# A two-block transformer kernel: the second key unit's copy-out moved ahead, eight vector products regrouped between VectorE and GpSimd, GpSimd's products cut into 512-column pieces

## The reference

```python
mod_lat = jnp.split(jax.nn.silu(c) @ w_ada[l] + b_ada[l], 6, axis=-1)
mod_ctx = jnp.split(jax.nn.silu(c_ctx)[None, :] @ w_ada[l] + b_ada[l], 6, axis=-1)
pl = project(modulate(rmsnorm(x, g_mix[l]), sh1, sc1), w_in[l], w_dec_up[l], b_dec[l])
pc = project(modulate(rmsnorm(ctx, g_mix[l]), sh1c, sc1c), w_in[l], w_dec_up[l], b_dec[l])
o_c, s_cf, s_cb = gla_bidir(pc[0], pc[1], pc[2], pc[4], pc[5], zeros_state, zeros_state)
o_l, _, _ = gla_bidir(pl[0], pl[1], pl[2], pl[4], pl[5], s_cf, s_cb)
mix_l = merge_branches(o_l, pl[3], pl[6], ...)
x = x + gt1[:, None, :] * mix_l
x = x + gt2[:, None, :] * swiglu(modulate(rmsnorm(x, g_ffn[l]), sh2, sc2), ...)
```

## Time and profile before

| | us |
|---|---|
| median of 3 runs | 1207.5 (1204.62 to 1208.31) |
| profiled execution, its own time | 1210.52 |
| span of the profiled execution | 1208.5 |
| TensorE matmul busy | 1135.7 (94%) |
| VectorE busy | 861.6 (71%) |
| ScalarE busy | 569.5 (47%) |
| GpSimd busy | 325.1 (27%) |

### The profile page before, as it was taken

One profiled execution on the slowest core, in us unless ns is written; L12 is line 12 of the kernel. 1 busy time (PEld: TensorE's weight loads), 2 busy tenths in 40 slices (PEclk: granted clock), 3 DMA queues, 4 the chain that ended last, 5 costly groups with the idle time before them and its releaser, 6 DMA issues.

```text
span 1208.5 us, 19055 instructions
## 1 busy us (share of the span) xinstructions
PE 1135.7 (94%) x7764; PEld 1027.4 (85%) x7764; DVE 861.6 (71%) x944; ACT 569.5 (47%) x729; POOL 325.1 (27%) x226
## 2 busy tenths in 40 slices
PE   2968999999999999999989999999999989999996
PEld 2968988999998988888878888889998989888885
DVE  1579474488678678787778887788666687755676
ACT  3464434443442464444455444446655635544452
POOL 4077563165756100000020000011257663000000
PEclk8988989999999899999989999999999999999999
DMA  9932645466785658777737777756954565656670
GB/s 288 295 129 90 194 131 164 121 216 213 235 284 170 227 171 277 243 249 247 281 132 266 253 248 249 263 165 197 296 178 148 187 206 174 209 180 203 212 258 35
DMA packets 192547, 250.28 MB, mean 207 GB/s; under 512 B 4859, under 2 KB 171966, under 8 KB 192350
## 3 DMA queue, kind: packets, MB, share of 16 engines
q1 hardware_dynamic: 183838, 216.92, 55.3%
q0 software_dynamic: 8640, 32.38, 7.9%
HBM read 248.23 MB, written 1.05 MB: 206 GB/s over the span
## 4 chain that ended last, share of the span: by engine, by line
PE 75%; DVE 14%; ACT 4%; issue 4%; SPq 2%; DMA 1%; POOL 0%; POOLq 0%; DVEq 0%; ACTq 0%
PE twin L1286 73%; DVE arena L1892 5%; DVE wlo L1892 4%; ACT arena L864 2%; DVE arena L1900 2%; ACT whi L864 1%; DVE X L1892 1%; DMA arena<-in_w_ada 1%; PE twin L1347 1%; DVE arena L2175 1%; SPq L512 1%; PE twin L1612 0%; DVE X L1900 0%; SPq L562 0%; DVE arena L1896 0%
## 5 line engine op out<-in xcount | busy, mean ns | idle before, releaser
L1286 PE MATMUL twin<-A_both,whi 128*128 128x256 f32 (+1 forms) x2208 | 580.1, 340 | 1.5 <-DVE arena L1892 1.1
L1892 DVE TENSOR_TENSOR wlo<-raw,whi 128x2048 fp32r<-128x2048 f32 x169 | 420.2, 2487 | 144.5 <-ACT whi L864 144.3
L1286 PE MATMUL twin<-A_both,wlo 128*128 128x256 f32 x1632 | 437.0, 281 | 0.0
L864 ACT ACTIVATE whi<-raw 128x2048 fp32r<-128x2048 f32 x169 | 323.2, 1912 | 209.2 <-PE twin L1286 209.2
L1286 PEld LDWEIGHTS twin<-A_both,whi 128*128 128x128 f32 x2208 | 371.3, 190 | 44.7 <-issue 6.9
L1286 PEld LDWEIGHTS twin<-A_both,wlo 128*128 128x128 f32 x1632 | 309.9, 190 | 11.4 <-DVE A_both L1892 0.6
L1286 PE MATMUL twin<-whi,A_both 128*128 128x256 f32 x640 | 124.5, 296 | 27.5 <-ACT arena L864 15.2
L864 ACT ACTIVATE arena<-arena 128x512 f32<-128x512 f32 (+7 forms) x132 | 70.1, 558 | 167.9 <-DVE arena L1892 132.9
L864 ACT ACTIVATE arena<-twin 128x512 f32<-128x512 f32 (+5 forms) x167 | 88.4, 555 | 116.6 <-PE twin L1286 85.7
L779 POOL TENSOR_TENSOR ada_raw<-ada_raw,arena 128x2048 f32<-128x2048 f32 x24 | 98.1, 4089 | 136.7 <-DMA ada_raw<-in_w_ada 136.7
L1286 PEld LDWEIGHTS twin<-whi,A_both 128*128 128x128 f32 x640 | 105.4, 202 | 29.7 <-issue 16.2
(11 more groups left out here) (134 smaller groups left out, 1213.6 us busy)
## 6 DMA issues: line engine op xcount, KB each, us to landing
raw<-in_w_in SPq DMA_DIRECT2D x48, 1024.0 KB, 5.7
raw<-in_ffn_w_in SPq DMA_DIRECT2D x44, 1024.0 KB, 5.1
ada_raw<-in_w_ada POOLq DMA_DIRECT2D x28, 1024.0 KB, 6.2
ada_raw<-in_w_ada SPq DMA_DIRECT2D x24, 1024.0 KB, 5.4
raw<-in_w_ffn_in SPq DMA_DIRECT2D x22, 1024.0 KB, 5.1
raw<-in_ffn_w_out SPq DMA_DIRECT2D x22, 1024.0 KB, 4.9
raw<-in_w_ffn_out SPq DMA_DIRECT2D x11, 1024.0 KB, 5.1
arena<-in_w_ada SPq DMA_DIRECT2D x8, 1024.0 KB, 11.6
```

The costliest lines, as they stand in the source:

```text
L864: return nc.scalar.activation(o, i, f, **kw)
L1286: return nc.tensor.matmul(o, l, r, start=start, stop=stop, **kw)
L1892: return nc.vector.tensor_tensor(o, x, y, op)
```

## The change

Five edits, all in block one.

1. ScalarE copies out unit 2 (`evac1(U_K + 1)`) in round 2, between `decays(1)` and `log_decays(2)`, no longer in round 3.
2. Pieces 0 and 1 of the modulation products go to VectorE (`ADA_DVE`), in its rounds 4 and 5.
3. GpSimd still loads piece 0 at the same place, then loads piece 1 when VectorE is through with piece 0, piece 2 when it is through with piece 1, and only then computes, pieces 2 to 7.
4. On GpSimd the product of a block-one piece is 4 instructions of 512 columns, and the first sum 2 of 512.
5. VectorE does `decayed_queries` behind the second `gla_step` of rounds 8 and 9, so behind `add_state`.

```diff
--- before.py
+++ after.py
@@ -120,7 +120,7 @@
 
 ADA_FFN = [n for n in range(len(ADA)) if NADA1 <= n < ADA_P2 or n >= ADA_LAST]
 ADA_MIX = [n for n in range(len(ADA)) if n not in ADA_FFN]
-ADA_DVE = [n for n in range(len(ADA)) if n in ADA_FFN or ADA_P2 <= n < ADA_P2 + 4]
+ADA_DVE = [n for n in range(len(ADA)) if n < 2 or n in ADA_FFN or ADA_P2 <= n < ADA_P2 + 4]
 ADA_POOL = [n for n in range(len(ADA)) if n not in ADA_DVE]
 
 LAST_STEPS = (0, NF - 4, NF - 3, NF - 2)
@@ -776,8 +776,16 @@
                 dst = acc[:, UC * ada_pos(n):UC * ada_pos(n) + UC]
                 pool.wait_ge(*ada_landing(n))
                 v = ada_raw
-                link(nc.gpsimd.tensor_tensor(v[:], v[:], c3[:, :, s:s + 1].to_broadcast([P, KD, UC]), ALU.mult))
-                link(nc.gpsimd.tensor_tensor(v[:, 0:4, :], v[:, 0:4, :], v[:, 4:8, :], ALU.add))
+                step = 2 if n < NADA1 else 8
+                for k in range(0, KD, step):
+                    ins = nc.gpsimd.tensor_tensor(v[:, k:k + step, :], v[:, k:k + step, :],
+                                                  c3[:, k:k + step, s:s + 1].to_broadcast([P, step, UC]), ALU.mult)
+                link(ins)
+                step = min(step, 4)
+                for k in range(0, 4, step):
+                    ins = nc.gpsimd.tensor_tensor(v[:, k:k + step, :], v[:, k:k + step, :], v[:, k + 4:k + 4 + step, :],
+                                                  ALU.add)
+                link(ins)
                 link(nc.gpsimd.tensor_tensor(v[:, 0:2, :], v[:, 0:2, :], v[:, 2:4, :], ALU.add))
                 nc.gpsimd.tensor_tensor(dst, v[:, 0, :], v[:, 1, :], ALU.add).then_inc(ada_sum, 1)
 
@@ -814,10 +822,11 @@
             norm(0)
             norm(1)
             load_ada(0)
-            pool.wait_ge(hlo_done, 16)
-            for n in range(8):
+            load_ada(1)
+            for n in range(2, 8):
+                load_ada(n)
                 adapt(n)
-                load_ada(n + 1)
+            load_ada(8)
             for t in range(TT):
                 pool.wait_ge(osq_done, t + 1)
                 root(orstd[:, 4 * t:4 * t + 4], oss[:, 4 * t:4 * t + 4], HV).then_inc(orstd_done, 1)
@@ -1049,6 +1058,7 @@
                 if u == U_K + 1:
                     decays(0)
                     decays(1)
+                    evac1(U_K + 1)
                     log_decays(2)
                     soft_part(2)
                 if u == U_V:
@@ -1247,8 +1257,9 @@
             split(2)
 
             for u in range(N1):
+                if u and u != U_K + 2:
+                    evac1(u - 1)
                 if u:
-                    evac1(u - 1)
                     split(u + 2)
                 gla_front(u)
                 gla_step(2 * (u - 1 - U_Q) + 1)
@@ -2228,8 +2239,6 @@
                 if u == U_V:
                     for g in range(4):
                         decayed_keys(g)
-                if u in (U_Q + 1, U_Q + 2):
-                    decayed_queries(u - U_Q - 1)
 
             def gla_step(slot):
 
@@ -2517,6 +2526,11 @@
                     split(u + 2)
                 gla_front(u)
                 gla_step(2 * (u - U_Q))
+                if u in (U_Q + 1, U_Q + 2):
+                    decayed_queries(u - U_Q - 1)
+                if u in (U_V + 1, U_V + 2):
+                    n = u - U_V - 1
+                    adapt(n, 0, acc[:, UC * ada_pos(n):UC * ada_pos(n) + UC], ADA[n][0])
                 if P1[u - 1][0] == "ch":
                     conv(P1[u - 1][1])
                 if P1[u - 2][0] == "ch":
```

## The result

| | before | after |
|---|---|---|
| median, us | 1207.9 (1204.62 to 1208.39, 4 runs) | 1195.62 (1195.08 to 1196.76, 4 runs) |
| profiled execution / its span | 1210.52 / 1208.5 | 1195.08 / 1193.2 |

A forecast was written before the change was run, and what follows sets the result against it. TensorE, busy 94% of the span, was taken as the bound, so only its waits and lower clock could pay. Gains of 14.0 + 6.2 + 2.3 = 22.5 us off 1207.5 gave 1185.0 us, range 1179 to 1193.

The forecast's parts named there:

- (a): Passes 0 and 1: with GpSimd quiet, the decay chain loses 7.6 us and `decays(1)` ends at 76.0 us.
- (b): Unit 2's copy ends at 77.1 us, so unit 4's 12.4 us wait and 2.0 us of half clock go.
- (c): Passes 2 and 3: a 3.9 us wait before unit 5 replaces 2.8 us, with 1.8 us of half clock behind it.
- (d): Unit 6: the 0.7 us wait goes, it starts at 109.5 us instead of 123.5; gain so far 14.0 us.
- (e): Pieces 0 and 1 on VectorE, rounds 4 and 5: about 4 us waiting for piece 1's load, cost nothing.
- (f): Round 8, query products behind state additions: the 2.8 us wait and 3.4 us of half clock go, 6.2 us.
- (g): 512-column GpSimd pieces: each costs 0.8 to 1.7 us more with nobody waiting; shorter VectorE holds gain 2.3 us.
- GpSimd comes late to the square roots: Rival, chance 0.05: GpSimd's later start delays the roots for `norm_heads` past 223.7 us; slower, say 1211 us.
- A new wait in rounds 8 and 9: Rival, chance 0.13: round 9's query products are held, a wait of 2 to 3 us plus half clock; 1191 us.
- The later waits close wholly: Rival, chance 0.10: the clock holds behind the 3.9 us wait and shorter pieces bring 4.9 us; 1180.6 us.
- Held by something else: Rival, chance 0.05: something other than GpSimd holds VectorE, so only the changed orders act; 1202.4 us.

The follow-up runs named there:

- e11: The changed kernel without the early copy of unit 2, which is copied out in round 3 again; 1196.38 us, ratio 0.9906.
- e7: The kernel before with only the early copy of unit 2 added; 1208.59 us, ratio 0.9996.
- e1: The changed kernel with GpSimd's products whole again, one instruction of 2048 columns and one sum of 1024; 1199.23 us, ratio 0.9927.
- e2: The changed kernel with only pieces 2 to 7 cut and pieces 8 to 15 whole; 1201.12 us, ratio 0.994.
- e3: The changed kernel with pieces 2 to 7 whole and only pieces 8 to 15 cut; 1192.52 us, ratio 0.9873.
- e9: The changed kernel with a third piece (piece 2) on VectorE, leaving GpSimd five ahead of the first square roots; 1188.18 us, ratio 0.9842.
- e10: The changed kernel with a third piece on VectorE and the second norm's roots ahead of GpSimd's last piece; 1186.53 us, ratio 0.9819.
- e12: The changed kernel with the query products ahead of the state additions again; 1199.53 us, ratio 0.9925.
- e6: The changed kernel with GpSimd's roots of the second norm ahead of its sixteenth piece instead of behind it; 1190.01 us, ratio 0.9859.
- e8: The kernel before with only pieces 0 and 1 on VectorE and GpSimd silent until they are done, products whole; 1200.01 us, ratio 0.9932.
- e4: The kernel before with only the cut of GpSimd's products into 512 columns; 1190.25 us, ratio 0.9858.

## Why the prediction was right or wrong

**(a) Quiet GpSimd: right.** The first chain ends at 74.66 us. `decays(1)`, forecast to end at 76.0 us, starts its exponentials at 74.77 and ends them at 76.02 us.

**(b) Earlier copy: right in its place, empty as a term.** Unit 4 starts at 80.8 us without a wait. But e11 has nearly the same time without it: then unit 4 waits 4.8 us and unit 5 nothing. With GpSimd active the copy alone is worth nothing either (e7).

**(c) Right: 3.7 us of wait for 3.9.** The second chain started at 84.18 us (forecast 84.4), its `split` at 93.69 (93.9). The 1.8 us of half clock did not come in this execution. In six of the seven other kernels that are the same up to there (e1, e2, e3, e9, e10, e12; not e6) the clock did fall behind it, so as a price it was fair.

**(d) and (e): right.** The lead at unit 8 is 15.9 us, forecast 14.0 plus the clock that held. Piece 0 took 3.61 us from 103.56 us, piece 1 waited 4.75 us for its load (about 4), and no unit waited for either.

**(f) Right mechanism and sum, but edit 5 was not needed for it.** The lead rose from 15.9 to 21.9 us, 6.0 for 6.2. That the order protects is shown with whole products: in e1 the pair is held 6.29 us behind the additions and TensorE does not wait, in e8 (which also lacks edit 1) it is held 6.88 us ahead of them and TensorE waits 2.8 us. But e12, without edit 5, has the same rise (14.9 to 20.9), and so have e4 (9.6 to 15.6) and e7 (-0.2 to 5.8), e7 even with whole products. In all three the pair of round 8 runs while GpSimd waits for a load. So a shift of a few us against GpSimd's pieces takes this wait away; whether the cut alone would, with the pair beside a product in round 8, no run shows (in round 9 of e12 the pair took 2.90 us and nobody waited).

**(g) is the step that failed, twice.** I wrote that a piece costs 0.8 to 1.7 us more "with nobody waiting", and the gain in exchange was put at 2.3 us between bounds of 0 and 4.9.

The cost: start-to-start was 17.6 us where I had 16.2 to 17.1, and 21.9 behind the roots, where before had 19.6 ((378.52 - 241.32) / 7) and e1's whole pieces 18.5 ((362.51 - 233.02) / 7). The row of pieces so reached both roots.

Up to the first root my base was wrong more than the price of the cut. The 15.4 us were one distance, the second shortest of before's seven, whose mean is (185.09 - 60.07) / 7 = 17.9 us; e1's whole pieces take (212.62 - 125.24) / 5 = 17.5 us. With 17.5 us in my own sum the last of six whole pieces ends at 124.6 + 5 x 17.5 + 9 = 221.1 us, 2.6 us ahead of the deciding point and not 9.1. So the late start of edit 3 used up the 41.75 us: e1 is late there too, and e9, with one piece fewer, has no such wait. What TensorE then waits is 1.1 and 1.4 us where these six pieces are whole (e1, e3) and 4.2 to 4.4 us where they are cut (after, e2, e6, e11, e12).

At the second norm the 23.62 us of idle time were used up by the late start and by the cut. The first of the eight products starts 8.5 us earlier than in before (232.81 against 241.32) where the lead at unit 45 is 26.7 us, which takes 18 us; seven distances of 2.3 us more take 16. e1, whole, has its 24.5 us back, and e6, with the root ahead of the last piece, has no long wait. Together the two waits took 5.7 + 6.2 = 11.9 us of lead. I had not read GpSimd's timeline beyond 300 us, where this second deadline stands.

The gain: from unit 22 on to unit 45 the lead rose by 26.7 - 16.2 = 10.5 us, and from unit 16 to 45 by 9.8 (15.6 to 25.4) in e4, against a fall in e1 and e2. That is the 2.5 us wait of the earlier trace rows and the 4.6 us for `A_both`, with their clock. My bound of 4.9 held the first and put the second, ahead of `mix_out`, at 1.5 us, for the same reason: the view of waits ended at 300 us.

In medians the two waits explain most of the miss: e10, which removes both (with a third piece on VectorE), is 9.1 us faster than after, and the forecast was missed by 10.2 us.

**The rest.** 5.3 us of lead went in block two, whose code is the same in both. From the copy of unit 113 to that of 145 it took 230.2 us in before's profile and 230.4 to 235.9 in the thirteen others. TensorE stood idle for 8.0 to 9.7 us there in all fourteen; what differs is the granted clock, 0.99 in before, e1 and e9, 0.98 to 0.96 in the others. No edit orders them (e6 232.8, e9 230.4, e10 235.9), so it is not put down to the change; but before has the shortest of the fourteen, so a small cost that all the edited kernels share isn't excluded. And before's profiled execution is 2.6 us above its own median and after's 0.5 below, which is why a lead of 15.2 us is a gain of 12.3 in the medians. The profiled executions of e4 and e10 lie 3.3 us below and 3.2 us above theirs: leads at unit 145 do not order the kernels, the medians do.

**The rivals.** "GpSimd comes late to the square roots" (0.05) named the right place and its deciding point: the last piece was to be done by 223.7 us and was done at 226.6. Its price, worked out only for the case that ends slower, hid that a lateness of 3 to 4 us was the likely form of it. That sum was off too: by its own terms the start-to-start for 246.2 us is (246.2 - 124.6 - 9) / 5 = 22.5 us, not 20.3. "A new wait in rounds 8 and 9" did not occur, and not in e12 with the old order either. "The later waits close wholly" did occur, for more than its 4.9 us. "Held by something else" is excluded by the short instructions.

The forecast's sum is what e10 reaches, which removes both new waits: 1208.6 - 1186.5 = 22.1 us against 22.5. That the numbers agree is in part luck: the gain of (g) was too small by 8 us, and of e10's lead of 29.3 us at unit 45 it lost 2.6 us at the second norm and 5.8 us in block two, which the forecast did not have.

**The rule of a page.** By the Trainium skill (SBUF — State Buffer, "Who interferes with whom") the later of the two engines waits for the whole instruction that holds the lock. The runs agree: the subtraction held 3.93 us in before took 1.37 us in e4, where the GpSimd instruction beside it took 1.03 us in place of 4.26. The rule was in the prediction, but only as the price of a hold; that shorter instructions on GpSimd alone would bring 17 us was not drawn from it.

## What to carry to other kernels

When an engine holds another for whole instructions, first cut the holder's instructions and measure that alone: here one edit made 17 us and left GpSimd's work where it had slack. When work of an engine off the critical path is moved later or made longer, write down every result that it delivers, up to the end of the block, with the idle time ahead of each (here 41.75 and 23.6 us), and take the new row against each of them, with the mean of all its distances and not with one of them (17.9 us here, not 15.4). And a copy moved ahead of a wait is worth nothing until the chain behind it is shorter too.

## What the runs showed of the hardware

The clock behind one and the same wait differed. Up to 96 us the changed kernel, e1, e2, e3, e6 and e12 run the same program, and TensorE stood still 3.7 us in each; from 95.8 to 100 us its mean granted clock was 1.00 in e6 and 0.62 in e2. e2_cut_2_7's windows, and e6_early_root's:

```profile
95.80:100.00 4.20, 4.19 (x23) 4.20 (x24) 4.20 (x11) 4.20 (x4) 0.00 (x0) 0.62 0.76 233
```

```profile
95.80:100.00 4.20, 4.20 (x37) 4.20 (x37) 4.20 (x12) 4.20 (x4) 0.00 (x0) 1.00 0.80 250
```

So a price of "half clock behind each wait" is right on average and not in the single case: at unit 8 the lead is 16.5 us in e6 and 14.8 in e2, 1.7 us apart in the same program.

A cut product is nearly as fast as a whole one when nothing disturbs it: 4.03 us for four of 512 columns against 3.61 for one of 2048, after, at 159.75 us. Beside a busy VectorE the four took up to 6.99 us (at 254.82 and 363.18 us) and the whole one up to 4.78 us (before, at 110.02 us), so GpSimd is held as well, and longer in all with four instructions. The Trainium skill (GPSIMD Engine Reference, "Elementwise — side-by-side cycle accounting") measures about 2.6 cycles for an element and gives no time there for the dispatch of one instruction; these rows show 0.4 us more for four instructions than for one, undisturbed.
